# The arena of a fused two-block transformer kernel moved from byte 114624 to byte 106496 of each partition

## What is computed

```
x = first_block(x, c, ctx, ...)     # 2 layers; x and ctx (256 tokens each) side by side;
                                    # adaptive modulation, h @ w_in (7168 columns), differential attention,
                                    # depthwise conv, merge, sqrelu MLP with D_FF = 4096.
                                    # In layer 1 the context only gives keys and values.
x = second_block(x, ...)            # layer 0: sliding-window attention + gated delta rule, MLP
                                    # layer 1: RG-LRU, MLP;  layer_norm after each

def sqrelu_mlp(h, w1, w2):
    return jnp.square(jax.nn.relu(h @ w1)) @ w2
```

## Time and profile before

| | |
|---|---|
| device time, median of 3 runs | 2089.11 us |
| the three runs | 2085.4, 2089.11, 2089.83 us |
| span of the profiled execution | 2089.1 us |
| time of the profiled execution beyond its span | none is given; the span equals the median to 0.1 us |
| busy share: PE, weight loads, DVE, ACT, POOL | 97%, 86%, 65%, 49%, 8% |
| PE's share of the chain that ended last | 88% |
| mean granted TensorE clock | 0.991 of full speed |
| HBM traffic | 292 MB read, 140 GB/s over the span |

### The profile page before, as it was taken

The page is one execution under the profiler, slowest core; times in us unless marked ns, Lnnn a source line. Parts: engine busy times, 40 slices in busy tenths (PEclk is TensorE's granted clock), DMA queues, the critical chain, the costliest instruction groups (busy, mean ns, idle before and its releaser), DMA issues.

```text
span 2089.1 us, 36236 instructions
## 1 busy us (share of the span) xinstructions
PE 2024.6 (97%) x13946; PEld 1789.9 (86%) x13946; DVE 1363.7 (65%) x2114; ACT 1019.1 (49%) x2014; POOL 162.3 (8%) x174
## 2 busy tenths in 40 slices
PE   6999999999999999999999999999999999999998
PEld 5899657888788888879967999999998989888897
DVE  5699688344565564577977667776766555886455
ACT  5475575324422322358457454445824444675443
POOL 0000000000000001000000002223120111000110
PEclk9999999999999999999999999999999999999999
DMA  7322374222222222233255545554302555443553
GB/s 287 122 82 102 122 283 161 81 101 101 81 83 98 100 100 83 98 108 135 83 203 217 179 147 181 185 192 176 115 21 82 181 181 188 184 164 137 191 183 121
DMA packets 40896, 294.56 MB, mean 141 GB/s; under 512 B 4544, under 2 KB 4544, under 8 KB 5456
## 3 DMA queue, kind: packets, MB, share of 16 engines
q1 hardware_dynamic: 40464, 290.73, 38.4%
q0 software_dynamic: 320, 2.26, 0.3%
HBM read 291.93 MB, written 1.05 MB: 140 GB/s over the span
## 4 chain that ended last, share of the span: by engine, by line
PE 88%; DVE 5%; ACT 4%; issue 1%; DMA 1%; SPq 0%; DVEq 0%; ACTq 0%
PE psum L652 21%; PE psum L654 21%; PE psum L653 20%; PE psum L1017 3%; PE psum L1021 3%; PE psum L1018 3%; PE psum L890 2%; PE psum L1224 2%; DVE weights_lo L1964 2%; PE psum L793 2%; PE psum L912 1%; PE psum L692 1%; PE psum L693 1%; PE psum L694 1%; ACT weights_hi L1363 1%
## 5 line engine op out<-in xcount | busy, mean ns | idle before, releaser
L1964 DVE TENSOR_TENSOR weights_lo<-raw_weights,weights_hi 128x2048 fp32r<-128x2048 f32 x225 | 512.6, 2291 | 163.1 <-ACT weights_hi L1363 162.7
L1363 ACT ACTIVATE weights_hi<-raw_weights 128x2048 fp32r<-128x2048 f32 x225 | 429.0, 1910 | 152.6 <-DMA raw_weights<-in_weights 133.1
L2043 DVE SCALAR_TENSOR_TENSOR xT<-psum,mods,xT 128x256 f32<-128x256 f32 x408 | 181.0, 479 | 199.9 <-PE psum L654 196.5
L652 PE MATMUL psum<-h_hi,weights_hi 128*128 128x512 f32 (+1 forms) x832 | 279.9, 336 | 0.1
L654 PE MATMUL psum<-h_lo,weights_hi 128*128 128x512 f32 (+1 forms) x832 | 279.8, 336 | 0.0
L653 PE MATMUL psum<-h_hi,weights_lo 128*128 128x512 f32 (+1 forms) x832 | 278.1, 334 | 0.0
L2840 POOL TENSOR_TENSOR ffsq<-ff 128x256 f32<-128x256 f32 (+1 forms) x128 | 118.2, 925 | 1592.1 <-ACT ff L1450 1107.6
L652 PE MATMUL psum<-weights_hi,h_hi 128*128 128x256 f32 x704 | 197.5, 280 | 0.0
L653 PE MATMUL psum<-weights_lo,h_hi 128*128 128x256 f32 x704 | 195.5, 278 | 0.0
L654 PE MATMUL psum<-weights_hi,h_lo 128*128 128x256 f32 x704 | 195.5, 278 | 0.0
L652 PE MATMUL psum<-g_hi,weights_hi 128*128 128x256 f32 x688 | 193.7, 282 | 0.0
(11 more groups left out here) (423 smaller groups left out, 4277.6 us busy)
## 6 DMA issues: line engine op xcount, KB each, us to landing
raw_weights<-in_weights SPq DMA_DIRECT2D x273, 1024.0 KB, 4.8
staged_x<-in_x_rows SPq DMA_DIRECT2D x1, 2048.0 KB, 10.0
masks<-in_masks POOLq DMA_DIRECT2D x1, 1152.0 KB, 6.8
ln_rows<-in_ln_rows POOLq DMA_DIRECT2D x1, 1024.0 KB, 6.8
out<-outrow SPq DMA_DIRECT2D x4, 256.0 KB, 2.1
rows<-in_rows SPq DMA_DIRECT2D x1, 584.0 KB, 9.7
consts<-in_consts SPq DMA_DIRECT2D x1, 388.0 KB, 3.8
cols<-in_cols SPq DMA_DIRECT2D x1, 306.0 KB, 2.8
```

What stands on the lines that cost most here:

```text
L652: mm(out, *pair(wh, vh), start=i == 0, stop=False)
L1363: f(w_hi[:, s, :], raw[:, s, :], ACT.Copy).then_inc(hi_done, 1)
L1964: tt_(w_lo[:, s, :], raw[:, s, :], w_hi[:, s, :].bitcast(F32), ALU.subtract).then_inc(lo_done, 1)
L2043: last = stt(xT[:, m, c], b[:, c], mods[:, l, which + m, v:v + 1], xT[:, m, c], ALU.mult, ALU.add)
```

## The change

Two numbers are changed.

```diff
         ARENA = 112 * 1024
-        arena_at = -(-nc.sbuf_base // 64) * 64
+        arena_at = -(-nc.sbuf_base // 128) * 128
...
-    nc = bacc.Bacc("TRN2", target_bir_lowering=False, num_devices=1)
+    nc = bacc.Bacc("TRN2", target_bir_lowering=False, num_devices=1, dynamic_dma_scratch_size=8192)
```

## The result

The changed kernel takes 2112.21 us (median of 2110.58, 2111.17, 2113.25 and 2116.19) where the kernel before took 2089.47 beside it (2085.4, 2089.11, 2089.83 and one odd execution of 5204.07, which is in this median and can't be in the ratio): 1.0117 times as long, 95% interval 1.01 to 1.0134. It is slower by 23 us, outside the predicted range of 2068 to 2095. Of the rivals it is B, slower, with its sign, about its size and its mark of 233 ns; it had a chance of 0.16.

What follows compares the result with a forecast made beforehand. TensorE, busy 97% of the span, was taken to bound the kernel. 2089.1 us + 0 for the arena's place + 0 for other engines - 0.2 for DMA gave 2088.9 us, range 2068 to 2095.

Steps and rivals of the forecast that it cites:

- B: TensorE's ring and arena reads collide more often: +18 us, 2107 us, marked by 233 ns at 512 columns; chance 0.16.
- What bounds the kernel: Whole kernel: TensorE, busy 97% of 2089.1 us, so only its pitch or a wait it feels could show.
- Part 1: Arena tiles standing on 0 instead of 448 modulo 512, read by TensorE: between 18 us less and 18 more, taken as 0.
- The +18 us: Upper end for the arena's new place: 9 us on 512-column arena tiles plus 9 us on streams moving weights.
- The step for 512-column arena tiles: Upward pitch step of 4.4 ns on 2016 fp32r matmuls moving 512 arena columns: 9 us at most.
- For moving weights 9 us: Upward pitch step of 4.4 ns on 2112 matmuls moving weights, if all were fast before: 9 us at most.
- The float32 rows: Float32 matmuls with both operands in the arena (275, 279 ns) or below it (280): the 64 bytes are worth nothing there.
- Parts 2 and 3: DVE, ACT and POOL at new places: 0; DMA landings and halved scratch: -0.2 us, range -1.2 to +0.2.
- the -0.2 taken: DMA transfers at the kernel's start and end: 0.2 us less, with -1.2 to +0.2 kept for the range.
- Rival A: The arena's place caused the slow pitch; its 256-column streams go to 113.4 ns, the kernel to 2071 us; chance 0.27.
- The argument against it: In the long MLP windows of 162 and 280 us, ring-arena distance takes many values, yet each stream keeps one pitch.
- The pages cited: Skill notes on TensorE spacing (215.8 and 109.2 ns) and SBUF's 16-byte lines, by which the new address does nothing.

Runs made afterwards that it cites:

- the first experiment: The changed kernel with the arena's rounding put back to 64 bytes, scratch still halved: 2089.68 us, ratio 1.0008 to the kernel before the change.

## Why the prediction was wrong

- **What bounds the kernel: right.** TensorE is at 97% in both kernels, and the loss is in its pitch.
- **Part 1, the price of the arena's place: wrong.** The step that failed is "I take 0", with the reason "whatever picks the pitch is then not the address alone". The sentence is true, and the conclusion doesn't follow. Two things pick the pitch: the distance modulo 256 bytes says which pitches a stream can have (at 256 columns 113.3 or 117.8 before, 118 to 120 after), and something else, in part the stream ahead, says which of them it takes. The earlier trace rows show the second at a fixed first; they say nothing on the price of changing the first. The term put at 0 measured 24 us of pitch, and the time grew by 23. The +18 us was no true bound either: it left out 576 of the 2592 arena matmuls of 512 columns and 240 of the 2352 of moving weights, and gave the 256-column arena tiles, at 117.8 already, no step up.
- **Its terms, one by one.** The step for 512-column arena tiles was taken on 2016 matmuls (9 us); it hit them and the 576 others of that width, at 3.9 ns, 10.1 us. For moving weights 9 us were put on 2112 matmuls, taken as all fast; of 2352 about 1600 had been fast, and the group paid 9.2. Not foreseen were 1.2 ns on the 256-column arena tiles, 5.9 us, and the gain of 1.1 on the 512-column weights.
- **The float32 rows, as evidence: wrong kind.** The earlier trace rows showed no price of place, and after the change they are as they were (both kinds of `ut` and `tIT` start 111.7 ns apart in either trace). But both operands of each of these matmuls moved together, which by the runs changes nothing even for fp32r, so they say nothing on the price of a changed distance. The prediction had noted that no fp32r row has both operands on one side, and let them count all the same.
- **Parts 2 and 3, the other engines and the DMA: right.** DVE 2291 ns as before, `staged_x` and `outrow` shorter by 0.3 and 0.1 us, near the -0.2 taken. In the changed kernel tile `w` lands 6.9 us after its issue, with no delay from the halved scratch, and the first experiment shows scratch and the 8 KB together to cost less than a measurement can tell.
- **Rival A: wrong way round.** The arena's place is a reason for the pitch, but the changed place took the last fast stretches away, and of the places tried in the whole kernel none gave 113.3 throughout. The gain that A looked for came in part with 128 bytes in the second block, not with the 64 of the change.
- **Rival B: right in sign and in that the distance decides; its collision is not shown.** Its 2107 us against 2112.21 are partly luck: its two steps, 9 us each, measured 10.1 and 9.2, and the 5.9 us of the 256-column arena tiles were not in it. The argument against it, that the distance takes many values and every stream keeps its pitch, was in fact half of the evidence for it: the distances differ by multiples of 512, and the runs show that only the remainder by 256 counts. The prediction wrote down that the 64 bytes "are not tried by that", and gave B 0.16 still. With "not tried" as the honest reading, 0 had no better claim than a step up or down.
- **The pages cited.** The Trainium skill (TensorE: Matmul & The Clock Gate, Back-to-back issue gap) gives N/2.4 ns plus about 2.5. The best values here are 226.7 and 113.3 ns, above the 215.8 and 109.2 estimated from it, at all of the distances tried. The Trainium skill (SBUF — State Buffer, the note on cachelines) has lines of 16 bytes; that a shift of 64 is then free was the prediction's inference, and the runs show that for a pair of tiles it is not.

What stays open: why 256 bytes, and what in the chip settles a stream on one of its pitches. The runs show a period and, nearly, a symmetry of moving and staying tile, which fits reads of the stream and of the next weight load that meet; the meeting itself no trace shows.

## What to carry to other kernels

Where TensorE reads a moving tile and loads the next weights with fp32r at every matmul, the distance between the two tiles modulo 256 bytes was worth up to 3% of the pitch at 512 columns (226.7 to 233.3 ns) and 6% at 256 (113.3 to 120.0), so moving one buffer by 64 bytes is a change to be timed, not tidying. Try the four remainders for each pair of tiles that a long stream uses, in the whole kernel, since a stream's pitch also depends on the one ahead of it. And when rows show a quantity varying at a fixed setting, that proves a second cause, not that the setting has none.

## What the runs showed of the hardware

- With high and low tiles at the same remainder (0, 64, 128 or 192), the pitch of alternating fp32r matmuls and weight loads takes few steady values: 113.3, 117.8, 118 to 119 and 120.0 ns for 256 columns, 226.7, 228.9 and 231 to 233.5 for 512, all at full clock. With different remainders there are more, from 113.3 to 121 and from 226.7 to 234.5.
- They depend on the distance of the moving and the staying tile modulo 256 bytes. Of these four remainders 0 is the best for 512 columns (226.7) and the worst for 256 (120.0); 128 never is the best.
- At remainders 64 and 192 a 256-column stream has two pitches at the same addresses, 113.3 and 117.8 ns, and past its entry keeps one of them. At remainder 64 a 512-column arena stream has two as well, 228.9 and 233.3.
